# Key scores one pair of heads at a time, one group behind, with the block choice and the gate norm's sums laid out anew

## The reference, cut to what matters

```python
def moba_attend(q, kb, vb, t, slopes):
    kbar = jnp.mean(kb.astype(jnp.float32), axis=2)
    g = jnp.einsum('hqd,hnd->hqn', qf.astype(jnp.float32), kbar)
    _, top = lax.top_k(g, min(MOBA_TOPK, NB))
    ...
    s = jnp.einsum('hqd,hqnkd->hqnk', qf, ks).astype(jnp.float32) - slopes[:, None, None, None] * dist
    p = jax.nn.softmax(s.reshape(H, q.shape[1], -1), axis=-1).reshape(s.shape)
...
vn = layernorm(jax.nn.gelu(v_a), ln_g, ln_b)      # 1024 columns: mean and variance over them
```

## Time and profile before

| what | before |
|---|---|
| median of 3 runs | 1266.81 us (1264.7 to 1268.0) |
| the profiled execution | 1269.21 us |
| its span | 1267.5 us |
| mean granted TensorE clock | 0.976 |
| PE busy | 1186.6 us (94%) |
| DVE / ACT / POOL busy | 715.2 / 564.7 / 316.5 us |
| key stage, from the first turn to the end of the last scores | 341.1 to 505.6 us of the span |

### The profile page before, as it was taken

The page is one execution under the profiler, slowest core; times in us unless marked ns, Lnnn a source line. Parts: engine busy times, 40 slices in busy tenths (PEclk is TensorE's granted clock), DMA queues, the critical chain, the costliest instruction groups (busy, mean ns, idle before and its releaser), DMA issues.

```text
span 1267.5 us, 23692 instructions
## 1 busy us (share of the span) xinstructions
PE 1186.6 (94%) x9344; PEld 1055.6 (83%) x9344; DVE 715.2 (56%) x1358; ACT 564.7 (45%) x715; POOL 316.5 (25%) x196
## 2 busy tenths in 40 slices
PE   5799999999999899999999988699999989999995
PEld 2589798878888778887888977599999989999994
DVE  2745555544545545534454445559999996682122
ACT  3323433333444435432233234557666756574442
POOL 1000000000000000200000003267777678606771
PEclk9899999999999899999999989799999999999997
DMA  9999899999887867999999986275848445454432
GB/s 299 337 313 343 280 323 320 377 357 343 298 304 259 278 208 262 288 375 305 345 374 331 306 307 215 77 248 159 282 151 294 137 134 183 142 175 156 160 117 91
DMA packets 236274, 324.87 MB, mean 256 GB/s; under 512 B 12365, under 2 KB 152461, under 8 KB 235245
## 3 DMA queue, kind: packets, MB, share of 16 engines
q1 hardware_dynamic: 233040, 312.78, 73.1%
q0 software_dynamic: 1936, 7.78, 2.1%
q10 hardware_dynamic: 1188, 2.79, 0.7%
HBM read 317.96 MB, written 7.06 MB: 256 GB/s over the span
## 4 chain that ended last, share of the span: by engine, by line
PE 71%; DVE 16%; DMA 5%; SPq 2%; issue 2%; ACT 2%; POOL 0%; ACTq 0%; DVEq 0%; POOLq 0%
PE PS L305 17%; PE PS L309 17%; PE PS L308 17%; DVE PS L1663 10%; PE PS L391 5%; PE PS L974 4%; PE PS L1002 3%; SPq L378 2%; PE PS L1211 2%; DMA XR<-in_ada_w 2%; DMA WRAW<-in_ab_w_out 2%; DVE WLO L299 1%; DMA ACTS<-in_x_sample 1%; ACT WHI L294 1%; PE PS L404 1%
## 5 line engine op out<-in xcount | busy, mean ns | idle before, releaser
L305 PE MATMUL PS<-HH,WHI 128*128 128x288 f32 x2176 | 665.6, 306 | 29.5 <-DVE HL L448 15.2
L309 PE MATMUL PS<-HH,WLO 128*128 128x288 f32 x2176 | 645.7, 297 | 0.0
L308 PE MATMUL PS<-HL,WHI 128*128 128x288 f32 x2176 | 645.6, 297 | 0.0
L305 PEld LDWEIGHTS PS<-HH,WHI 128*128 128x128 f32 x2176 | 413.0, 190 | 52.9 <-issue 37.4
L294 ACT ACTIVATE WHI<-WRAW 128x1024 fp32r<-128x1024 f32 x272 | 284.1, 1057 | 372.3 <-PE PS L309 300.6
L308 PEld LDWEIGHTS PS<-HL,WHI 128*128 128x128 f32 x2176 | 413.5, 190 | 0.0
L309 PEld LDWEIGHTS PS<-HH,WLO 128*128 128x128 f32 x2176 | 412.5, 190 | 0.0
L299 POOL TENSOR_TENSOR WLO<-WRAW,WHI 128x1024 fp32r<-128x1024 f32 x116 | 278.7, 2422 | 237.8 <-ACT WHI L294 237.8
L299 DVE TENSOR_TENSOR WLO<-WRAW,WHI 128x1024 fp32r<-128x1024 f32 x156 | 190.7, 1224 | 174.1 <-ACT WHI L294 172.7
L1663 DVE SCALAR_TENSOR_TENSOR PS<-ACTS,CWT,PS 128x288 f32<-128x288 f32 x448 | 192.5, 516 | 0.0
L1639 ACT ACTIVATE ACTS<-ACTS 128x1088 f32<-128x1088 f32 x32 | 70.4, 2200 | 60.8 <-DVE ACTS L1661 34.6
(11 more groups left out here) (263 smaller groups left out, 763.7 us busy)
## 6 DMA issues: line engine op xcount, KB each, us to landing
XR<-in_ada_w SPq DMA_DIRECT2D x192, 512.0 KB, 8.8
WRAW<-in_ab_w_in SPq DMA_DIRECT2D x112, 512.0 KB, 7.5
WRAW<-in_c_w_in SPq DMA_DIRECT2D x96, 512.0 KB, 3.6
XR<-in_cache_b_k SPq DMA_DIRECT2D x128, 256.0 KB, 4.9
XR<-in_cache_b_v SPq DMA_DIRECT2D x128, 256.0 KB, 5.4
WRAW<-in_ab_w_out SPq DMA_DIRECT2D x32, 512.0 KB, 10.2
WRAW<-in_c_w_out SPq DMA_DIRECT2D x32, 512.0 KB, 3.2
ACTS<-in_x_prompt ACTq DMA_DIRECT2D x2, 1024.0 KB, 7.9
```

The source lines that it names most:

```text
L305: first = pe.matmul(out, whi, HH[:, k, :], start=start, stop=False)
L308: pe.matmul(out, whi, HL[:, k, :], start=False, stop=False)
L309: return pe.matmul(out, wlo, HH[:, k, :], start=False, stop=stop)
```

## The change

- Scores are computed for one pair of heads per call: 32 calls of 8 matmuls in place of 16 calls of 16. The pair 0 (or 2) is called after group 6 (or 14), in the middle of a chunk, the pair 1 (or 3) after group 0 of the next half; each call waits for the save of the turn one group before the last. KT's two halves come free by pairs.
- On DVE the penalties and the maximum move behind saves and are spread: two additions each at two places of (4, 1), the maximum at (4, 2). The exponential moves to (4, 3), the turns of its result to (5, 0), (5, 1), (5, 2).
- The gate norm: POOL, which did nothing in this stage, folds the eight chunks of VA to two before the sum for the mean, and squares and folds them before the sum for the variance: 3 additions, then 4 multiplications and 3 additions of 128 x 576. PE makes 2 matmuls with ones for each sum in place of 8; ACT's eight squares go. The subtraction of the mean is cut into four of 576 columns, at (6, 1), (6, 2) and (6, 3), the mean is taken at (6, 0) and the variance with its reciprocal at (7, 2), the root at (7, 3).

The diff, cut to its core:

```diff
         def k_save(eng, u, c, g4):
             g, hh, j = 16 * u + 4 * c + g4, 2 * (c // 2) + g4 // 2, 2 * (c % 2) + g4 % 2
             eng.wait_ge(kt_tr, g + 1)
-            if 2 * u + c // 2:
-                eng.wait_ge(ks_head, 2 * u + c // 2)
+            if 4 * u + hh >= 2:
+                eng.wait_ge(ks_head, 4 * u + hh - 1)
...
-        def k_scores(pe, u, half):
-
-            pe.wait_ge(kt_a, 8 * u + 4 * half + 4)
-            pe.wait_ge(kt_d, 8 * u + 4 * half + 4)
-            if half == 0:
+        def k_scores(pe, u, hh):
+
+            pe.wait_ge(kt_a, 8 * u + 4 * (hh // 2) + 3 + hh % 2)
+            pe.wait_ge(kt_d, 8 * u + 4 * (hh // 2) + 3 + hh % 2)
...
-            for hh in (2 * half, 2 * half + 1):
-                for h2 in range(2):
-                    h = 2 * hh + h2
-                    for j in range(4):
-                        last = pe.matmul(PS[32 * j:32 * j + 32, M0, 0:BLOCK], QM[:, j, h, :], KT[:, hh % 2, j, h2, :],
-                                         start=h == 0, stop=h == HEADS - 1)
+            for h2 in range(2):
+                h = 2 * hh + h2
+                for j in range(4):
+                    last = pe.matmul(PS[32 * j:32 * j + 32, M0, 0:BLOCK], QM[:, j, h, :], KT[:, hh % 2, j, h2, :],
+                                     start=h == 0, stop=h == HEADS - 1)
             last.then_inc(ks_head, 1)
...
-                    if u == 4 and c == 2:
-                        probs_turn(pe, 0, 0)
-                    if u == 4 and c == 3:
-                        probs_turn(pe, 0, 1)
-                    if c % 2:
-                        k_scores(pe, u, c // 2)
-                    if u == 5 and c == 0:
-                        probs_turn(pe, 0, 2)
-                    if u == 5 and c == 1:
-                        pe.wait_ge(g_act, 4)
+                        if g == 0 and n > 16:
+                            k_scores(pe, (n - 17) // 2, 2 * ((n - 17) % 2) + 1)
+                        if g == 6:
+                            k_scores(pe, u, c - 1)
+                    if u == 5 and c < 3:
+                        probs_turn(pe, 0, c)
+                    if u == 5 and c == 3:
+                        pe.wait_ge(va_sum, 3)
                         pe.wait_ge(s_ptc, 3)
-                        for k in range(GC):
-                            last = pe.matmul(PS[:, M1, 0:R], ONES[:], VA[:, k, :], start=k == 0, stop=k == GC - 1)
+                        for x in range(2):
+                            last = pe.matmul(PS[:, M1, 0:R], ONES[:], VAS[:, x, :], start=x == 0, stop=x == 1)
                         last.then_inc(g_mean, 1)
-                    if (u, c) in ((6, 1), (6, 2), (6, 3), (7, 0)):
-                        x = 4 * (u - 6) + c - 1
-                        for k in (2 * x, 2 * x + 1):
-                            pe.wait_ge(s_sq, k + 1)
-                            pe.matmul(PS[:, M1, 0:R], ONES[:], SQ[k % 2], start=k == 0, stop=k == GC - 1).then_inc(s_sqmm, 1)
+                    if (u, c) == (7, 1):
+                        pe.wait_ge(s_sq, 7)
+                        for x in range(2):
+                            last = pe.matmul(PS[:, M1, 0:R], ONES[:], VAS[:, x, :], start=x == 0, stop=x == 1)
+                        last.then_inc(s_sqmm, 1)
+            k_scores(pe, 7, 3)
...
-        def va_square(act, k):
-            act.wait_ge(g_ln, k // 4 + 1)
-            if k >= 2:
-                act.wait_ge(s_sqmm, k - 1)
-            act.activation(SQ[k % 2], VA[:, k, :], ACT.Square).then_inc(s_sq, 1)
+        VAS = A(2304 + 1152, 2 * R).rearrange("p (c r) -> p c r", r=R)
+        VAT = SCR[:, R:3 * R].rearrange("p (c r) -> p c r", r=R)
+
+        def va_sums(pool):
+
+            pool.wait_ge(s_own, 2)
+            for x in range(1, 4):
+                pool.wait_ge(g_act, x + 1)
+                if x > 1:
+                    pool.wait_ge(va_sum, x - 1)
+                pool.tensor_tensor(VAS, VA[:, 0:2, :] if x == 1 else VAS, VA[:, 2 * x:2 * x + 2, :], ALU.add).then_inc(va_sum, 1)
+            pool.wait_ge(g_mean, 1)
+            for x in range(4):
+                pool.wait_ge(g_ln, x + 1)
+                va = VA[:, 2 * x:2 * x + 2, :]
+                if x == 0:
+                    pool.tensor_tensor(VAS, va, va, ALU.mult).then_inc(s_sq, 1)
+                else:
+                    if x > 1:
+                        pool.wait_ge(s_sq, 2 * x - 1)
+                    pool.tensor_tensor(VAT, va, va, ALU.mult).then_inc(s_sq, 1)
+                    pool.wait_ge(s_sq, 2 * x)
+                    pool.tensor_tensor(VAS, VAS, VAT, ALU.add).then_inc(s_sq, 1)
...
-                    if (u, c) == (4, 1):
+                    if (u, c) == (4, 3):
                         row_exp(act, 0)
-                    if (u, c) in ((4, 3), (5, 0), (5, 1)):
-                        probs_save(act, 0, 4 * (u - 4) + c - 3)
-                    if u == 6:
-                        va_square(act, 2 * c)
-                        va_square(act, 2 * c + 1)
-                    if (u, c) == (7, 2):
+                    if u == 5 and c < 3:
+                        probs_save(act, 0, c)
+                    if (u, c) == (7, 3):
                         root(act, 2)
...
-            dve.wait_ge(ks_head, 2 * u + 2)
+            dve.wait_ge(ks_head, 4 * u + 4)
...
+        def rows_add(dve, first):
+            for n in (first, first + 1):
+                blk = SROW[:, n * BLOCK:(n + 1) * BLOCK]
+                dve.tensor_scalar(blk, blk, PEN[:, n:n + 1], None, ALU.add).then_inc(s_pen, 1)
+
         def rows_max(dve, b):
-            for n in range(NBLK):
-                blk = SROW[:, n * BLOCK:(n + 1) * BLOCK]
-                last = dve.tensor_scalar(blk, blk, PEN[:, n:n + 1], None, ALU.add)
-            link(dve, "dve", last)
+            dve.wait_ge(s_pen, 4 * b + 4)
...
-        def va_centre(dve, half):
-            va = VA[:, 4 * half:4 * half + 4, :]
-            dve.tensor_tensor(va, va, bc(RB.unsqueeze(1), [P, 4, R]), ALU.subtract).then_inc(g_ln, 1)
+        def va_centre(dve, x):
+            va = VA[:, 2 * x:2 * x + 2, :]
+            dve.tensor_tensor(va, va, bc(RB.unsqueeze(1), [P, 2, R]), ALU.subtract).then_inc(g_ln, 1)
...
-                        dve.wait_ge(ks_head, 8)
+                        dve.wait_ge(ks_head, 16)
                         mask_q(dve, 1)
+                    k_save(dve, u, c, 1)
                     if (u, c) == (4, 1):
-                        rows_max(dve, 0)
-                    k_save(dve, u, c, 1)
+                        rows_add(dve, 0)
+                    if (u, c) == (6, 1):
+                        va_centre(dve, 0)
+                    if (u, c) == (6, 3):
+                        va_centre(dve, 3)
                     if c % 2 == 0:
                         lo(dve, 67 + 2 * u + c // 2)
                     k_save(dve, u, c, 3)
+                    if (u, c) == (4, 1):
+                        rows_add(dve, 2)
+                    if (u, c) == (4, 2):
+                        rows_max(dve, 0)
                     if u and c == 0:
                         scores_take(dve, u - 1)
                         if u == 4:
                             choose_blocks(dve, 0)
                     if u in (2, 4, 6) and c == 2:
                         gate_b(dve, u // 2 - 1)
-                    if (u, c) == (4, 3):
+                    if (u, c) == (5, 0):
                         dve.wait_ge(s_exp, 1)
                         dve.reciprocal(RZ[:, 0:1], ZSUM)
-                    if (u, c) == (5, 2):
+                    if (u, c) == (6, 0):
                         dve.wait_ge(g_mean, 1)
                         link(dve, "dve", dve.tensor_scalar(RB, PS[:, M1, 0:R], 1.0 / DA, None, ALU.mult))
-                    if (u, c) == (5, 3):
-                        va_centre(dve, 0)
-                    if (u, c) == (6, 0):
-                        va_centre(dve, 1)
-                    if (u, c) == (7, 1):
-                        dve.wait_ge(s_sqmm, GC)
-                        dve.wait_ge(g_ln, 2)
+                    if (u, c) in ((6, 1), (6, 2)):
+                        va_centre(dve, c)
+                    if (u, c) == (7, 2):
+                        dve.wait_ge(s_sqmm, 1)
+                        dve.wait_ge(g_ln, 4)
...
                     choose_blocks(dve, 1)
+                    rows_add(dve, 0)
+                    rows_add(dve, 2)
                     rows_max(dve, 1)
...
-            pool.wait_ge(ks_head, 16)
+            pool.wait_ge(ks_head, 32)
...
             rows_pool(pool)
+            va_sums(pool)
             gmlp_pool(pool)
```

More of the change, by code:

```diff
@@ L208, in trunk @@
         ada_cp, ada_tr, ada_done = sem("ada_copied"), sem("ada_turned"), sem("ada_done")
-        s_sq, s_sqmm = sem("squares_ready"), sem("squares_summed")
+        s_sq, s_sqmm, va_sum = sem("squares_ready"), sem("squares_summed"), sem("va_chunks_added")
+        s_pen = sem("penalty_added")
         s_hf, s_hh, s_hl = sem("rows_normalised"), sem("input_hi"), sem("input_lo")
```

(8 more changed lines are left out.)

## The result

The changed kernel takes 1252.39 us (median of 4 runs, 1249.4 to 1256.99) against 1267.4 of the kernel before beside it; the ratio is 0.9892, with an interval of 0.9872 to 0.9912. That is 11 to 16 us off, 13.7 in the middle. Forecast were 10.8 us off and 1256.0 us. The profiled execution took 1251.29 us, its span 1249.6.

| | before | changed |
|---|---|---|
| span | 1267.5 | 1249.6 |
| key stage | 164.5 | 152.1 |
| the rest of the span | 1103.0 | 1097.5 |

The account below looks back on a forecast made before the run. PE, busy for 94% of the span, was taken to bound the kernel. The terms summed to -10.8 us: 1258.4 from the profiled 1269.2, or 1256.0 from the median of 1266.8; range 1251.5 to 1262.

Parts of the forecast that it names:

- Scores by pairs: Key stage score calls on PE: 13 waits of 0.50 us go, 16 added calls cost 0.27 each, together -2.2 us.
- Sums with ones: Gate norm on PE: both sums shrink from 8 chunk pairs to 2, -5.8 us; shorter wait behind the silu at u = 6, -0.6.
- The root: At (7, 2): the root no longer delays a save of ACT, -0.2 us, an estimate.
- The choice of blocks: At (4, 1) and (4, 2): shorter PE waits for DVE's saves, -1.7 us, and no half clock afterwards, -2.7.
- the old stall: PE's wait at (4, 1) in the kernel before, for a save behind choice, penalties and maximum; counted as 3.6 us.
- The reciprocal: At (7, 2): moved on DVE behind `lo` and two saves, it makes PE wait for the save of turn 13, +1.15 us.
- Centring and POOL beside DVE: At (6, 2): `gate_b` and a centring ahead of turn 13's save, +0.3 us; `lo` held up by POOL's addition, +1.0.
- Late saves at many places: Rival: DVE is late for half of the 31 score calls, losing 0.3 us each, 1261 us; chance 0.14.
- the clock falling at (4, 1): Rival: 1.3 us of wait and short breaks still lower the clock, 2.7 us or more back, 1259 to 1260; chance 0.10.
- slower: Rival: every score call keeps a wait because saves come later; with waits of 0.6 us in 31 calls, 1275; chance 0.03.
- More gain: Rival: waits at (4, 2), (6, 2) and (7, 2) are shorter than counted; without their 3 us, 1253; chance 0.17.

Follow-up runs that it names:

- single_heads: The changed kernel with 63 score calls of 4 matmuls for one head in place of 32 of 8: key stage 160.4 us, ratio 0.9981.
- improved: halves_behind with `lo` in odd quarters, penalties behind both saves of (4, 1), squares' sum and reciprocal earlier, last scores later, page numbers earlier: key stage 151.8 us, ratio 0.9890.
- pool_busy: The changed kernel with 50 more POOL additions on memory of its own, through u = 2 to 4: key stage 162.3 us, ratio 0.9967.
- halves_in_place: The changed kernel with scores again in 16 calls of 16 matmuls behind the last group of a half: key stage 156.2 us, ratio 0.9939.
- penalties_first: The changed kernel with all four penalties and the maximum again ahead of the save of turn 5 at (4, 1): key stage 155.4 us, ratio 0.9937.
- sums_only: The kernel before with only the gate norm's sums folded on POOL, two matmuls each, ACT's squares gone: key stage 158.3 us, ratio 0.9952.
- halves_behind: The changed kernel with 16 score calls of 16 matmuls, each one group behind, in place of 32: key stage 151.8 us, ratio 0.9902.

## Why the prediction was right

The median, 1252.4 us, fell into the range, 0.9 us above its lower end, and below the 1254 to 1258 that I held most likely: the interval of the ratio, 11 to 16 us, begins just above the sum's 10.8. Step by step, in the key stage, where I had 153.7 us and 152.1 came:

- **Scores by pairs, -2.2.** The mechanism held to the hundredth: entry 0.09, call 1.00, next group 0.90, no wait (margin 0.34 us) in 27 of 32 calls. The price of 0.27 us for a call, put together from rows of three places, is confirmed by single_heads (8.3 us for 31). Undone by itself in the changed kernel, this part is worth 4.1: 15 waits go there and not 13, a little longer than the 0.50 counted, and one of them is 0.9.
- **Sums with ones, -5.8 and -0.6.** Alone they gave 6.2. In the changed kernel the wait behind the silu is 0.51 us at u = 6 too. POOL's ten instructions took 13.5 us (14 expected) and nothing waited for their end.
- **The root, -0.2.** Held: turn 14 of u = 7 came 1.02 us after turn 13 before and 0.83 now.
- **The choice of blocks, -1.7 and -2.7.** Waits of 1.07 and 0.49 us came where 1.3 and 0.6 were expected, and the clock stayed up. The sum used 3.6 for the old stall, which is the loss from start to start where the row says 3.44. Undone, this part costs 3.4, not 4.4: with a wait of the same length the half clock lasted 3.4 us there, 6.8 before.
- **The reciprocal, +1.15.** 0.93 measured, 0.99 from start to start.
- **Centring and POOL beside DVE, +0.3 and +1.0.** The term that was mis-sized: 0.6 us from start to start (0.17 in the list) in place of 1.3. POOL's addition did meet `lo`, but it had been running for 0.8 us, so `lo` lost 0.5 and not the whole 1.4. The mechanism is real: in improved it made the centring and `lo` together 1.8 us longer, with a wait of 2.4 behind them, and pool_busy is 10 us longer for it, slow clock included.
- **The rivals.** Late saves at many places, the clock falling at (4, 1), and slower did not come. "More gain" (1253) is nearest to what happened, and its reason holds for a part: of the 3 us of waits at (4, 2), (6, 2) and (7, 2), 2.1 came from start to start, so 0.9 were too much. The other 0.7 by which the stage is shorter than my sum are spread over small differences that I do not take apart.
- **Outside the stage.** I gave back nothing and took nothing there; the profiles agree, within a scatter of 6 us that no step of mine had. The launch gained 13.7 us where the stage gained 12.4; the interval holds both, so nothing more is shown.

## What to carry to other kernels

A call that waits for the last save before it can be put one piece of independent work later; what that gives is the wait less the cost of every additional change between full and quarter-width matmuls, which was 0.27 us here against a wait of 0.50. Before splitting a call to get it off a wait, try moving it whole and moving what then stands in front of the saves. On an engine that serves a tight loop, put long and patient work (penalties, a maximum, a centring) behind the instruction that the loop waits for, and never where another engine's reads can hold it up.

## What the runs showed of the hardware

**DVE beside POOL.** Instructions of DVE that read SBUF were held up while POOL worked: `lo` 1.74, 1.97 and 2.43 in place of 1.21, the centring 1.31 in place of 0.75, and, which I had not expected, those with one input in SBUF too: penalties 0.88 in place of 0.35. It goes both ways: where a `lo` began first in pool_busy (376.2 us), POOL's addition behind it took 2.01 in place of 1.15. Not every instruction is touched: the maximum took 1.24 us in both, and copies from PSUM kept their 687 ns through 64 saves, 31 of them beside POOL. The Trainium skill says as much (SBUF — State Buffer, Who interferes with whom): two SBUF inputs contend, and among one-input operations those that run in a 2-port mode. The times here agree with it, though no run shows in which mode the penalties ran.

**The clock.** Waits of PE of 1.07 and 1.12 us (the changed kernel, halves_in_place) left it at 2.4 GHz. With waits of 2.39 (improved), 3.41 (penalties_first) and 3.46 us (sums_only) came 3.4 us at 1.2 GHz, which began 0.4 to 1.4 us after the wait. With 3.44 (before) and 4.41 us (pool_busy) came 6.8, which began inside the wait, 1.5 and 1.2 us before its end. So a wait of 3.4 us cost 3.4 us of half clock in two profiles and 6.8 in another, and no run shows what decides between them.

**A wait that the list does not show.** In halves_behind 0.24 us of PE in 13 of the 16 halves were in no row of who waited for whom, since the modelled end of the matmul before covered them; the distance of starts has them. In the changed kernel the list has 0.17 of the 0.6 us at (6, 3).
